# The low part's product ahead of the wide one in one block of every wide chunk

## The chip, the core and the metric

One Trainium2 chip, one NeuronCore of it. The kernel computes a whole two-part model block in one launch. The metric is the device time of a launch in microseconds; the median of the runs is quoted.

## The reference, cut to what matters

Two transformer-like blocks over 256 tokens of width 1024, all in fp32: a first one (gated feed forward of width 2816, latent and stick-breaking attention, a second gated feed forward, a gated projection) and a second one (short convolution, squared-ReLU feed forward of width 4096, sparse attention, another such feed forward, a final norm). What counts here are the dense products with weights:

```python
def swiglu(u, w_in, w_out):
    a, b = jnp.split(u @ w_in, 2, axis=-1)
    return (jax.nn.silu(a) * b) @ w_out

def squared_relu_mlp(h, w1, w2):
    return jnp.square(jax.nn.relu(h @ w1)) @ w2
```

They are wanted at nearly fp32 precision. The kernel reaches it by splitting: each fp32 operand is a high part (rounded to the fp32r format) and a low part (the rest), and a product is high x high + high x low + low x high.

## The kernel before, in words

**Weights.** All dense weights are packed into chunks of 128 partitions x 2048 fp32 (1 MB). Chunks are loaded in order into a ring of three slots `raw` by DMA from SyncE. ScalarE copies a chunk to its high part (`w_hi`, L438), VectorE subtracts to get the low part (`w_lo`, L858, semaphore `lo_split`), TensorE uses the chunk and counts `chunk_used` up, and ScalarE may overwrite the slot. Both parts lie in the tensor `w_hl`.

**Blocks.** A chunk that feeds the feed forwards holds 16 blocks of 128 x 128 weights. A block is either a `product` (L1625 to L1629): three matmuls of 256 columns, namely weights high with x high, weights high with x low, weights low with x high; or a `wide` (L1631 to L1635): one matmul of 512 columns, weights high with x high and x low side by side (L1634, 256 columns each, into a whole PSUM bank), and one of 256 columns, weights low with x high (L1635), added to the bank's first half. The two halves of the bank are added later by ScalarE and VectorE. Every matmul has its own weight load. `wide_low_first` (L1637 to L1641) is the same block with the two matmuls exchanged; both add to what an earlier block began, so it is never the first block of a bank.

**Wide chunks.** An up-chunk (`up`, L1706) makes two output tiles t = 0, 1 over eight input tiles k; the loops run over t and then k. In the first chunk of a stage the input x is only just being made, so `up` goes in four pieces, each behind a wait for the x piece (`op_lo`), with two k for each t in a piece. There are 22 up-chunks in ffn1 and ffn2 and 16 in mlp0 and mlp1. The second chunk of the program has a function of its own, `up_halves` (L1731), which uses `thirds` for four of its blocks. A down-chunk (`feed_forward`, L1791 to L1805) holds 16 consecutive blocks of a long list (output tile o outside, hidden tile f inside); there are 11 in ffn1, 11 in ffn2 and 16 in mlp0. mlp1's down projection (`last_down`) is built otherwise, from three 512-column matmuls (L1824 to L1826). Three output projections (`w_out`, `conv_out`, `nsa_out`) have four chunks each, three of them wide and one in the product form (`OUT_BANKS`, `NSA_OUT_BANKS`: a second entry of 0 marks the product form); they run through `out_tile`, `out_chunk`, `two_pairs` and, in the sparse attention, `out_piece` (L2221).

**Where the low part goes first now.** In the first chunk of `w_out` and `conv_out` (L1697), in the first up-chunk of ffn2, mlp0 and mlp1 (L1724), each at t = 0, k = 1, and in the first chunk of `nsa_out` at k = 4 (L2229). The instructions ahead of the three-matmul products and behind them are in the order of the code; TensorE executes its matmuls in that order. The waits stand at the head of a chunk (`arrived`, for `lo_split`, which is behind the whole low part) and of a piece, none between the two matmuls of a block.

## Time and profile before

| what | us |
|---|---|
| median of 3 runs (1194.53 to 1196.97) | 1195.65 |
| the profiled execution | 1195.6 |
| its span, first to last instruction | 1193.8 |
| TensorE busy in it | 1184.0 |
| VectorE, ScalarE, GpSimd busy | 859.2, 644.1, 226.9 |

The profile is of one execution. A matmul's start is recorded and its end modelled, so distances between starts are the firm numbers. The timeline gives starts to 0.01 us. PE is TensorE, PEld its weight loads, DVE VectorE, ACT ScalarE, POOL GpSimd.

### The profile page before, as it was taken

The page shows a single profiled execution, that of the slowest core. Times are in us where ns is not written, and L with a number is a line of the kernel's source. Part 1 is how long each engine was busy: PE and PEld are TensorE (multiplying, and loading weights), DVE is VectorE, ACT ScalarE, POOL GpSimd, SP SyncE. Part 2 cuts the span into 40 slices and gives each one's busy share as a digit, 9 for nine tenths or more (in the row PEclk, how much of TensorE's full clock was granted, in tenths as well). Part 3 has the DMA queues.
Part 4 walks back from the last instruction along what each step waited for, and adds up shares of the span by engine and source line. Part 5 has one row for each costly group of instructions (what it writes and reads, how often), then busy time and mean ns, then how long its engine had stood idle before and what let it go on. Part 6 is the DMA issues. An engine that isn't in the chain of part 4 may idle for free.

```text
span 1193.8 us, 19183 instructions
## 1 busy us (share of the span) xinstructions
PE 1184.0 (99%) x7641; PEld 1055.1 (88%) x7641; DVE 859.2 (72%) x1178; ACT 644.1 (54%) x860; POOL 226.9 (19%) x115
## 2 busy tenths in 40 slices
PE   9999999999999999999999999999999999999997
PEld 6888889988899888888999988888899978888886
DVE  6877767788868877766788786656578777766353
ACT  6655454465655755544643455444446784555432
POOL 1443301000000334310000024520000250455001
PEclk9999999999999999999999999999999999999999
DMA  8655555953245554555545555555576305555550
GB/s 319 212 180 198 186 177 187 275 209 107 106 151 180 178 208 177 194 194 182 177 161 186 187 204 206 179 197 192 181 278 233 121 19 177 186 202 178 184 202 36
DMA packets 31567, 218.03 MB, mean 183 GB/s; under 512 B 3584, under 2 KB 3856, under 8 KB 6272
## 3 DMA queue, kind: packets, MB, share of 16 engines
q1 hardware_dynamic: 29712, 210.07, 50.2%
q0 software_dynamic: 1488, 6.05, 1.8%
q8 instruction: 58, 0.95, 0.3%
q10 hardware_dynamic: 288, 0.79, 0.2%
q14 instruction: 21, 0.17, 0.0%
HBM read 215.82 MB, written 4.22 MB: 184 GB/s over the span
## 4 chain that ended last, share of the span: by engine, by line
PE 93%; DVE 4%; DMA 2%; ACT 1%; issue 1%; SPq 0%; DVEq 0%; ACTq 0%
PE bank L1634 38%; PE bank L1635 19%; PE bank L1627 7%; PE bank L1628 7%; PE bank L1629 7%; PE bank L1826 2%; PE bank L1825 2%; PE bank L1824 2%; DVE w_hl L858 1%; DMA raw<-weights 1%; PE bank L2081 1%; ACT w_hl L438 1%; PE bank L1975 0%; DMA par<-small 0%; PE bank L1755 0%
## 5 line engine op out<-in xcount | busy, mean ns | idle before, releaser
L858 DVE TENSOR_TENSOR w_hl<-raw,w_hl 128x2048 fp32r<-128x2048 f32 x194 | 444.0, 2289 | 134.1 <-ACT w_hl L438 133.2
L438 ACT ACTIVATE w_hl<-raw 128x2048 fp32r<-128x2048 f32 x195 | 370.5, 1902 | 135.8 <-PE bank L1635 46.6
L1634 PE MATMUL bank<-x_hl,w_hl 128*128 128x512 f32 x905 | 315.2, 394 | 0.2 <-DVE w_hl L1077 0.2
L377 POOL TENSOR_TENSOR hidden<-hid_f,hidden 128x256 fp32r<-128x256 f32 (+1 forms) x76 | 189.6, 2494 | 517.7 <-ACT hidden L521 306.0
L1635 PE MATMUL bank<-x_hl,w_hl 128*128 128x256 f32 x905 | 251.9, 278 | 0.0
L1634 PE MATMUL bank<-hidden,w_hl 128*128 128x512 f32 x608 | 210.9, 393 | 0.0
L1634 PEld LDWEIGHTS bank<-x_hl,w_hl 128*128 128x128 f32 x905 | 169.6, 187 | 39.1 <-DVE x_hl L908 0.7
L1635 PEld LDWEIGHTS bank<-x_hl,w_hl 128*128 128x128 f32 x905 | 170.4, 188 | 0.2
L1635 PE MATMUL bank<-hidden,w_hl 128*128 128x256 f32 x608 | 169.0, 278 | 0.0
L1634 PE MATMUL bank<-y_hl,w_hl 128*128 128x512 f32 x445 | 155.3, 395 | 0.0
L1627 PE MATMUL bank<-x_hl,w_hl 128*128 128x256 f32 x528 | 151.2, 286 | 0.1
L1629 PE MATMUL bank<-x_hl,w_hl 128*128 128x256 f32 x528 | 149.4, 283 | 0.0
L1628 PE MATMUL bank<-x_hl,w_hl 128*128 128x256 f32 x528 | 149.4, 283 | 0.0
L499 ACT ACTIVATE second<-bank 128x512 f32<-128x512 f32 (+1 forms) x100 | 54.4, 544 | 173.5 <-PE bank L1635 173.4
L1634 PEld LDWEIGHTS bank<-hidden,w_hl 128*128 128x128 f32 x608 | 113.9, 187 | 26.1
L1635 PE MATMUL bank<-y_hl,w_hl 128*128 128x256 f32 x445 | 123.6, 278 | 0.0
L1635 PEld LDWEIGHTS bank<-hidden,w_hl 128*128 128x128 f32 x608 | 114.4, 188 | 0.0
L1627 PEld LDWEIGHTS bank<-x_hl,w_hl 128*128 128x128 f32 x528 | 101.2, 192 | 2.0 <-issue 1.1
L1628 PEld LDWEIGHTS bank<-x_hl,w_hl 128*128 128x128 f32 x528 | 101.3, 192 | 0.1
L1629 PEld LDWEIGHTS bank<-x_hl,w_hl 128*128 128x128 f32 x528 | 101.3, 192 | 0.0
L1634 PEld LDWEIGHTS bank<-y_hl,w_hl 128*128 128x128 f32 x445 | 83.5, 188 | 19.2 <-issue 0.2
L958 DVE TENSOR_TENSOR t_ab<-bank,second 128x512 f32<-128x512 f32 x76 | 52.4, 690 | 64.2 <-ACT second L499 64.1
(397 smaller groups left out, 1713.6 us busy)
## 6 DMA issues: line engine op xcount, KB each, us to landing
raw<-weights SPq DMA_DIRECT2D x197, 1024.0 KB, 4.9
bias_skew<-bias_rows POOLq DMA_DIRECT2D x1, 3072.0 KB, 28.6
gate_or_bias<-bias_skew POOLq DMA_DIRECT2D x1, 2048.0 KB, 10.3
h<-x_t SPq DMA_DIRECT2D x2, 512.0 KB, 5.6
con<-consts SPq DMA_DIRECT2D x1, 769.5 KB, 12.7
raw<-weights ACTq DMA_DIRECT2D x1, 512.0 KB, 5.1
raw<-weights SPq DMA_DIRECT2D x1, 512.0 KB, 7.5
sv<-last_gain POOLq DMA_DIRECT2D x1, 512.0 KB, 4.0
```

Source lines behind the costliest of these rows:

```text
L377: nc.gpsimd.tensor_tensor(hidden[:, at, 1, :], src, hidden[:, at, 0, :].bitcast(F32), ALU.subtract).then_inc(hid_lo, 1)
L438: nc.scalar.activation(dst, src, ACT.Copy).then_inc(hi_split, 1)
L499: nc.scalar.activation(dst, src, ACT.Copy).then_inc(second_out, 1)
L858: V.tensor_tensor(w_lo[:, s, :], raw[:, s, :], w_hi[:, s, :].bitcast(F32), ALU.subtract).then_inc(lo_split, 1)
L958: V.tensor_tensor(t_ab[:, :, :], bank[:, s:s + 2, 0:S], second[:, j % 2, :, :], ALU.add).then_inc(ab_ready, 1)
L1627: mm(out_, w_hi[:, s, c:c + m], x[:, 0, :], start=start, stop=False, **kw)
L1628: mm(out_, w_hi[:, s, c:c + m], x[:, 1, :], start=False, stop=False, **kw)
L1629: return mm(out_, w_lo[:, s, c:c + m], x[:, 0, :], start=False, stop=stop, **kw)
L1634: mm(out_, w_hi[:, s, c:c + m], x, start=start, stop=False, **kw)
L1635: return mm(out_[:, 0:S], w_lo[:, s, c:c + m], x[:, 0, :], start=False, stop=stop, **kw)
L1824: mm(o, a, wh, start=f == 0, stop=False)
L1825: mm(o, a, wl, start=False, stop=False)
```

## The change

`wide` gets a flag `low_first`. With it the block issues the 256-column product with the low part first and the 512-column one behind it. The separate function goes, and the special places in `two_pairs`, `up` and `out_piece` with it. The flag is set in one block of every wide chunk: at t = 0, k = 1 in the up-chunks and output projections, at the second block of each down-chunk. `up_halves` does not set it.

```diff
--- before.py
+++ after.py
@@ -1628,17 +1628,14 @@
                 mm(out_, w_hi[:, s, c:c + m], x[:, 1, :], start=False, stop=False, **kw)
                 return mm(out_, w_lo[:, s, c:c + m], x[:, 0, :], start=False, stop=stop, **kw)
 
-            def wide(out_, s, c, m, x, start, stop):
+            def wide(out_, s, c, m, x, start, stop, low_first=False):
 
                 kw = dict(skip_group_check=True)
+                if low_first:
+                    mm(out_[:, 0:S], w_lo[:, s, c:c + m], x[:, 0, :], start=False, stop=False, **kw)
+                    return mm(out_, w_hi[:, s, c:c + m], x, start=False, stop=stop, **kw)
                 mm(out_, w_hi[:, s, c:c + m], x, start=start, stop=False, **kw)
                 return mm(out_[:, 0:S], w_lo[:, s, c:c + m], x[:, 0, :], start=False, stop=stop, **kw)
-
-            def wide_low_first(out_, s, c, m, x):
-
-                kw = dict(skip_group_check=True)
-                mm(out_[:, 0:S], w_lo[:, s, c:c + m], x[:, 0, :], start=False, stop=False, **kw)
-                return mm(out_, w_hi[:, s, c:c + m], x, start=False, stop=False, **kw)
 
             def thirds(out_, s, c, m, x, start, stop):
 
@@ -1673,7 +1670,8 @@
                 if banks[1] == 0:
                     return product(bank[:, banks[0], t * S:(t + 1) * S], s, k * 256 + t * P, P, x[:, k, :, :],
                                    start and t == 0, stop, skip_group_check=True)
-                return wide(bank[:, banks[0] + t * banks[1], :], s, k * 256 + t * P, P, x[:, k, :, :], start, stop)
+                return wide(bank[:, banks[0] + t * banks[1], :], s, k * 256 + t * P, P, x[:, k, :, :], start, stop,
+                            t == 0 and k == 1)
 
             def out_chunk(banks, s, x):
 
@@ -1694,9 +1692,6 @@
                                 pe.wait_ge(op_lo, PC[pieces] + p + 1)
                             for t in range(2):
                                 for k in range(KT // n * p, KT // n * (p + 1)):
-                                    if j == 0 and t == 0 and k == 1 and banks[j][1] > 0:
-                                        last = wide_low_first(bank[:, banks[j][0], :], c % RING, 256, P, x[:, 1, :, :])
-                                        continue
                                     last = out_tile(banks[j], (c + j) % RING, t, k, x, k == 0, k == KT - 1)
                         if b == n:
                             last.then_inc(chunk_used, 1)
@@ -1709,7 +1704,7 @@
                     for t in range(2):
                         for k in range(KT):
                             last = wide(bank[:, 2 * slot + t, :], s, k * 256 + t * P, P, x[:, k, :, :], k == 0,
-                                        k == KT - 1)
+                                        k == KT - 1, t == 0 and k == 1)
                     return last
                 n = NP[pieces]
                 for p in range(n):
@@ -1721,11 +1716,8 @@
                             arrived(1)
                     for t in range(2):
                         for k in range(KT // n * p, KT // n * (p + 1)):
-                            if t == 0 and k == 1 and not first:
-                                last = wide_low_first(bank[:, 2 * slot, :], s, 256, P, x[:, 1, :, :])
-                                continue
                             last = wide(bank[:, 2 * slot + t, :], s, k * 256 + t * P, P, x[:, k, :, :], k == 0,
-                                        k == KT - 1)
+                                        k == KT - 1, t == 0 and k == 1)
                 return last
 
             def up_halves(slot, x):
@@ -1798,7 +1790,8 @@
                         pe.wait_ge(hid_lo, b + f * UPS[stage] // nf + 1)
                     if f == 0 and o >= 5:
                         pe.wait_ge(h_upd, upd + o - 3)
-                    ins = wide(bank[:, DOWN_BANKS[o], :], c % RING, i % 16 * P, P, hidden[:, f, :, :], f == 0, ended)
+                    ins = wide(bank[:, DOWN_BANKS[o], :], c % RING, i % 16 * P, P, hidden[:, f, :, :], f == 0, ended,
+                                   i % 16 == 1)
                     if i % 16 == 15:
                         ins.then_inc(chunk_used, 1)
                     elif ended:
@@ -2226,9 +2219,6 @@
                 pe.wait_ge(op_lo, PC["o_nsa"] + p + 1)
                 for t in range(2):
                     for k in range(KT // n * p, KT // n * (p + 1)):
-                        if j == 0 and t == 0 and k == 4:
-                            last = wide_low_first(bank[:, NSA_OUT_BANKS[j][0], :], c % RING, 4 * 256, P, y_hl[:, 4, :, :])
-                            continue
                         last = out_tile(NSA_OUT_BANKS[j], c % RING, t, k, y_hl, k == 0, k == KT - 1)
                 if p == n - 1:
                     last.then_inc(chunk_used, 1)
```

## Rows read from the trace of the kernel before

**Rows 1.** The page's head: span, busy times, the 40 slices, granted clock (tenths)

```profile
span 1193.8 us, 19183 instructions
...
PE 1184.0 (99%) x7641; PEld 1055.1 (88%) x7641; DVE 859.2 (72%) x1178; ACT 644.1 (54%) x860; POOL 226.9 (19%) x115
...
PE   9999999999999999999999999999999999999997
...
PEclk9999999999999999999999999999999999999999
```

**Rows 2.** The page's chain of waits, by engine and line, and TensorE's list of waits

```profile
PE 93%; DVE 4%; DMA 2%; ACT 1%; issue 1%; SPq 0%; DVEq 0%; ACTq 0%
PE bank L1634 38%; PE bank L1635 19%; PE bank L1627 7%; PE bank L1628 7%; PE bank L1629 7%; PE bank L1826 2%; PE bank L1825 2%; PE bank L1824 2%; DVE w_hl L858 1%; DMA raw<-weights 1%; PE bank L2081 1%; ACT w_hl L438 1%; PE bank L1975 0%; DMA par<-small 0%; PE bank L1755 0%
...
PE bank L1853 <- POOL relb L365: 2.3, 1, 2.3
```

**Rows 3.** The page's groups of instructions: the wide block's matmul by moving operand

```profile
L1634 PE MATMUL bank<-x_hl,w_hl 128*128 128x512 f32 x905 | 315.2, 394 | 0.2 <-DVE w_hl L1077 0.2
...
L1634 PE MATMUL bank<-hidden,w_hl 128*128 128x512 f32 x608 | 210.9, 393 | 0.0
...
L1634 PE MATMUL bank<-y_hl,w_hl 128*128 128x512 f32 x445 | 155.3, 395 | 0.0
```

**Rows 4.** One source line (L1640, low part ahead): its matmuls, ns min/median/max, first and last start

```profile
L1640 PE MATMUL bank<-x_hl,w_hl x3: 282/285/286, 365.2 to 1009.1; 128*128 128x256 f32 x3
...
L1640 PE MATMUL bank<-y_hl,w_hl x3: 285/285/386, 387.6 to 988.8; 128*128 128x256 f32 x3
```

**Rows 5.** TensorE's timeline (start us, duration us), ffn1's up-chunks, steady

```profile
60.34 0.39 PE L1634 MATMUL bank<-x_hl,w_hl 128*128 128x512 f32 x1
60.57 0.28 PE L1635 MATMUL bank<-x_hl,w_hl 128*128 128x256 f32 x1
...
132.45 0.39 PE L1634 MATMUL bank<-hidden,w_hl 128*128 128x512 f32 x1
```

**Rows 6.** TensorE's timeline, first chunk of the output projection `w_out`, with the form

```profile
364.87 0.40 PE L1634 MATMUL bank<-x_hl,w_hl 128*128 128x512 f32 x1
...
365.22 0.29 PE L1640 MATMUL bank<-x_hl,w_hl 128*128 128x256 f32 x1
365.34 0.40 PE L1641 MATMUL bank<-x_hl,w_hl 128*128 128x512 f32 x1
365.58 0.40 PE L1634 MATMUL bank<-x_hl,w_hl 128*128 128x512 f32 x1
...
370.44 0.39 PE L1634 MATMUL bank<-x_hl,w_hl 128*128 128x512 f32 x1
```

**Rows 7.** TensorE's timeline, last chunk of `w_out` (products) and first of ffn2

```profile
381.54 0.28 PE L1627 MATMUL bank<-x_hl,w_hl 128*128 128x256 f32 x1
...
383.32 0.28 PE L1627 MATMUL bank<-x_hl,w_hl 128*128 128x256 f32 x1
...
387.28 0.40 PE L1634 MATMUL bank<-y_hl,w_hl 128*128 128x512 f32 x1
...
392.86 0.38 PE L1763 MATMUL bank<-sq,ones 128*128 128x256 f32 x1
```

**Rows 8.** TensorE's timeline, chunk 0 of ffn1, second and third block

```profile
10.05 0.40 PE L1634 MATMUL bank<-x_hl,w_hl 128*128 128x512 f32 x1
...
10.40 0.39 PE L1634 MATMUL bank<-x_hl,w_hl 128*128 128x512 f32 x1
```

**Rows 9.** TensorE's timeline, last down projection, 512-column matmuls in a row

```profile
1100.76 0.39 PE L1824 MATMUL bank<-w_hl,hidden 128*128 128x512 f32 x1
...
1101.44 0.39 PE L1824 MATMUL bank<-w_hl,hidden 128*128 128x512 f32 x1
```

**Rows 10.** TensorE's timeline, mlp1's first chunk, and the instruction after it

```profile
1008.74 0.40 PE L1634 MATMUL bank<-x_hl,w_hl 128*128 128x512 f32 x1
...
1014.38 0.38 PE L1763 MATMUL bank<-sq,ones 128*128 128x256 f32 x1
```

## Prediction

> **What bounds the kernel now.** I read the head of the page first: TensorE is busy 1184.0 of 1193.8 us, its busy row has 9 in every slice but the last, and the granted clock is at the 2.4 GHz level all along [rows 1]. The chain of waits says the same of the end: 93% of it is TensorE, and 57% is the two lines of the wide block alone; the list of waits has a single long one for TensorE, 2.3 us at the start [rows 2]. So TensorE never stands idle for data, nearly every nanosecond put on or taken off its stream moves the end, and no other engine can take the bound for a change of less than a per cent. The costs of this change must be read from the distances between starts of matmuls, not from busy times, because the ends are modelled and a busy TensorE can still be in a slower rhythm.
>
> The groups of instructions give the number of wide blocks in the usual order: 905 + 608 + 445 = 1958 [rows 3]; the low-first form stands six times (three and three) [rows 4].
>
> The steady rhythm: the low matmul starts 0.23 us after the wide one, and 13 chunks of 16 blocks lie between 60.34 and 132.45 us: 72.11 / 13 = 5.547 us a chunk, 0.3467 us a block [rows 5]. At 2.4 GHz 512 + 256 columns are 0.320 us; 0.0267 is left, 0.0133 for each matmul. ScalarE and VectorE split a chunk and update tiles beside all of this, and the rhythm does not move, so I take it for TensorE's own.
>
> **The change, part by part.** (a) No instruction is added or removed. Weights, moving operands, banks, waits and increments are the same; in one block of a chunk two neighbours change places. The wait for the chunk's low split stands ahead of the whole chunk, so the low part is there when it is read first: no new wait, and no transfer or queue is moved. Cost 0; what hides it is that wait itself, and if it came late (by row it never does) both orders would wait alike.
>
> (b) The count. Afterwards the form stands in 21 of ffn1's 22 up-chunks (the second goes through `up_halves`, not touched), in 22, 16 and 16 of the other stages, in 11 + 11 + 16 down-chunks and in 3 wide chunks of each of three output projections: 75 + 38 + 9 = 122, against six now. 116 are new. One of the six moves, in the attention's output projection, from the fifth input tile to the second; it stays one block, and I give the move nothing (bounds: the price of one block either way, 0.03 us).
>
> (c) The price of one. The order high, low, high, low becomes high, low, low, high, high, low: a short-to-long and a long-to-short transition give way to a short-to-short and a long-to-long one. Both new transitions exist elsewhere, in steady streams. Short-to-short, in the three-matmul product: 33 matmuls from 383.32 to 387.28 us, 0.120 each [rows 7]. Long-to-long, in the last down projection: 0.68 for three, 0.227 each [rows 9]. The sum is 0.347, which is what the pair takes now. That is the lower end: **0 a block**. I exclude a gain as a term of the sum since all three streams have the same 0.0133 over the pure columns; a gain is a rival below.
>
> The upper end is a chunk that has the form now. From 364.87 to 370.44 us is 5.57 [rows 6], from 387.28 to 392.86 is 5.58 [rows 7]; two more, at 669.88 and 692.30, repeat it. The mean, 5.575, is **0.028 over** the steady chunk. In the rows the surplus sits right behind the swap: the low matmul put first takes 0.12, the long one behind it 0.24 until the next long one, where 0.227 is the steady distance [rows 6]. But these four all follow a stream of three-matmul products, and such a border has a cost of its own. In the other direction it gives time back: from 381.54 (the last wide chunk has ended) to 387.28 us are 48 matmuls in 5.74 us, where 48 x 0.120 is 5.76, so 0.02 is gained [rows 7]. If entering costs what leaving gives, 0.008 is left for the swap. A start without the form, chunk 0 behind its wait, shows a second block of 0.35 against 0.347, next to nothing for entering [rows 8]; then the swap bears it all. So 0.008 to 0.028 by this, 0 by the transitions. I take **0.012**, near the border read backwards, since that is the same border, and a little above it for the 0.24 us directly at the swap.
>
> Sum: 116 x 0.012 = 1.4 us. All of it lies on the path, as TensorE is the path. The slow rhythm described next is not counted as cured. The profiled execution took 1195.6 us (1193.8 span and 1.8 around it), and the median of the three is 1195.65, so the sum stands against either: **1197.0 us**.
>
> A rule to weigh: in the steady product stream, where every matmul has its own weight load, the distance is 0.120 us, so a load costs no more than that beside a 256-column matmul [rows 7]. The Trainium skill, "TensorE: Matmul & The Clock Gate", section "LDWEIGHTS (loading the stationary operand)", gives columns / 1.2 ns for a load, for 128 columns some 107 ns (an estimate), which would just fit under a 256-column matmul in either order; by it the swap is free and the time 1195.6 us. The chunks with the form do not bear that out in full.
>
> **The rivals.** About 0.2% (2.4 us) is what a measurement of this kernel can tell from no change.
> - *Order is free* (the steady streams). 0 x 116: 1195.6. For it: three streams with one overhead. Against it: the four chunks at 5.575. Chance 0.20.
> - *The swap bears the whole surplus* (ends on the slower side). Place: the two or three long matmuls after each swap. 116 x 0.028 = 3.2 us, 1198.8. It passes 0.2% from 0.021 a block on. For it: chunk 0 enters without a surplus. Against: leaving gains 0.02. Chance 0.18.
> - *The swap tips TensorE into the slow rhythm.* The chunk from 1008.74 to 1014.38 took 5.64, 0.093 over the steady one, though it holds the form [rows 10]; about four chunks in a row there run so, and the stream ahead of it was slow already. If swaps set it off for good it is 122 x 0.093 = 11.3 us, 1207; if in a third of the chunks, 3.8 us, 1199.4. For it: two of the six blocks of now stand in slow stretches. Against: both stretches were slow before the block, and four blocks are followed by the steady rhythm. Chance 0.12.
> - *A better rhythm.* Curing the slow chunks seen gives 4 x 0.093 = 0.4 us, not measurable. Over 0.2% faster takes 1.2 ns off each of 1964 blocks, below the 0.0133 that no steady stream here undercuts, or other executions with much more of the slow rhythm. About 1192.5. Chance 0.10.
> - *The change does not do what it says*: a block that is skipped. The count (b) would show it; it costs nothing, and is part of the free case.
>
> **How the numbers follow.** The forecast, small cost, has 0.40; most of it ends within 0.2% (up to 0.021 a block, 1198.0). Same: nearly all of 0.40 and 0.20, less the tails, 0.55. Slower: 0.18, 0.12 and a tail of the forecast, 0.33. Faster: 0.12. The range takes in the free case and the full surplus, with the run-to-run spread of 1 us below, and the slow rhythm in up to a third of the chunks above: 1194.2 to 1199.8.
>
> **What would show it.** Counts of the form: 122 and a line of 512 columns with 1842 blocks beside it. TensorE's share unchanged, and its waits too. Each chunk of the up and down stages from its first start to the next's: 5.547 (free), 5.559 (forecast), 5.575 (full surplus), 5.64 (slow rhythm). The prediction is wrong if that chunk is outside 5.547 to 5.575, and wrong in its idea if time comes or goes in stages without wide blocks, or if TensorE begins to wait.

## The result, and the profile after

The changed kernel is slower. Its median is 1207.8 us (six runs, 1205.56 to 1208.74) against 1196.07 for the kernel before (six runs, 1194.53 to 1196.98): a ratio of 1.0089, interval 1.0075 to 1.0104. The forecast of 1197.0 and its range (up to 1199.8) are missed; the time is the one that the rival of the slow rhythm gave, 1207.

The page of the changed kernel: its head, and the shares of the engines in the chain of waits.

```profile
span 1206.4 us, 19183 instructions
...
PE 1197.3 (99%) x7641; PEld 1061.5 (88%) x7641; DVE 859.2 (71%) x1178; ACT 644.3 (53%) x860; POOL 226.9 (19%) x115
...
PEclk9999999999999999999999999999999899999999
...
PE 99%; DVE 0%; ACT 0%; POOL 0%; issue 0%; DVEq 0%; POOLq 0%
```

Against [rows 1] the span is 12.6 us longer, TensorE is busy 13.3 us longer with the same 7641 matmuls, and VectorE and GpSimd are busy exactly as long as before. TensorE's list of waits still has one line, as in [rows 2]:

```profile
PE bank L1846 <- POOL relb L365: 2.4, 1, 2.4
```

So no new wait took the time. Next, the wide block's long matmul among the page's groups, and the line of the swapped low product (ns min/median/max, first and last start). They answer to [rows 3, 4].

```profile
L1637 PE MATMUL bank<-x_hl,w_hl 128*128 128x512 f32 x852 | 303.7, 398 | 0.0
...
L1637 PE MATMUL bank<-hidden,w_hl 128*128 128x512 f32 x570 | 203.0, 399 | 0.0
...
L1637 PE MATMUL bank<-y_hl,w_hl 128*128 128x512 f32 x420 | 150.0, 399 | 0.0
```

```profile
L1635 PE MATMUL bank<-x_hl,w_hl x56: 278/282/285, 10.2 to 1105.3; 128*128 128x256 f32 x56
...
L1635 PE MATMUL bank<-hidden,w_hl x38: 282/282/283, 134.8 to 874.8; 128*128 128x256 f32 x38
...
L1635 PE MATMUL bank<-y_hl,w_hl x28: 278/283/285, 390.8 to 1008.7; 128*128 128x256 f32 x28
```

The count is as predicted: 56 + 38 + 28 = 122 swapped blocks, 852 + 570 + 420 = 1842 in the usual order. What is new is the mean of the *unswapped* ones, 398 and 399 ns where it was 393 to 395. The change did not touch these blocks, and yet most of the time was lost on them. TensorE's timeline shows it (start us, duration us), a chunk well inside ffn1's up-chunks, and two later chunk starts:

```profile
66.61 0.40 PE L1637 MATMUL bank<-x_hl,w_hl 128*128 128x512 f32 x1
66.85 0.28 PE L1638 MATMUL bank<-x_hl,w_hl 128*128 128x256 f32 x1
66.97 0.28 PE L1635 MATMUL bank<-x_hl,w_hl 128*128 128x256 f32 x1
67.09 0.40 PE L1636 MATMUL bank<-x_hl,w_hl 128*128 128x512 f32 x1
67.32 0.40 PE L1637 MATMUL bank<-x_hl,w_hl 128*128 128x512 f32 x1
...
72.26 0.40 PE L1637 MATMUL bank<-x_hl,w_hl 128*128 128x512 f32 x1
...
128.79 0.40 PE L1637 MATMUL bank<-x_hl,w_hl 128*128 128x512 f32 x1
```

From 66.61 to 128.79 us are 11 chunks: 62.18 / 11 = 5.653 us, where [rows 5] give 5.547. The recorded starts are finer than the timeline's two digits, and taken in ns they show repeating patterns. From each start to the next, h for a 512-column matmul and l for a 256-column one:

| name in the text below | pattern, ns | a block | a chunk of 16 |
|---|---|---|---|
| one-block rhythm | h230 l117 | 346.7 | 5.547 |
| two-block rhythm | h231 l113, h233 l117 | 346.7 | 5.547 |
| slow rhythm, of three blocks | h241 l120, h236 l113, h233 l117 | 353.3 | 5.653 (or 5.661, 5.649, 5.650 in turn) |

The kernel before runs nearly all its wide chunks in one of the first two. In the changed one, 101 chunks of the four feed forwards are in the third: all from the fifth chunk on in ffn1, and from the fourth on in ffn2, mlp0 and mlp1. The trace shows the way in, at the second chunk of a stretch (27.05 us; the distances in ns are h230 l117, swap l118 h233, then h230 l114 h232 l118 **h241 l120**):

```profile
27.05 0.39 PE L1637 MATMUL bank<-x_hl,w_hl 128*128 128x512 f32 x1
...
27.40 0.28 PE L1635 MATMUL bank<-x_hl,w_hl 128*128 128x256 f32 x1
27.52 0.40 PE L1636 MATMUL bank<-x_hl,w_hl 128*128 128x512 f32 x1
27.75 0.39 PE L1637 MATMUL bank<-x_hl,w_hl 128*128 128x512 f32 x1
```

At the swap itself next to nothing is lost: from 27.05 to 27.75 us two blocks take 0.70, near their 0.693. The slow rhythm begins two blocks on and then holds; the next chunk's swap does not break it.

**Where the 12.6 us are.** ffn1 and ffn2, before and after, as TensorE's busy time and clock in their windows (the columns: window, its length, busy time and count of PE, PEld, DVE, ACT, POOL, clock granted, DMA share, GB/s). Before:

```profile
9.60:193.50 183.90, 183.87 (x1063) 162.02 (x1064) 139.75 (x172) 105.26 (x134) 49.00 (x22) 1.00 0.59 210
387.30:570.80 183.50, 183.50 (x1061) 160.43 (x1060) 136.79 (x169) 102.57 (x128) 49.92 (x22) 1.00 0.54 190
```

After:

```profile
9.70:196.60 186.90, 186.90 (x1064) 162.49 (x1063) 139.93 (x172) 105.13 (x133) 49.00 (x22) 1.00 0.58 206
390.40:577.20 186.80, 186.80 (x1060) 162.18 (x1059) 137.17 (x169) 102.56 (x128) 49.93 (x22) 1.00 0.53 186
```

The clock is granted in full in all four, and the same work takes 3.1 us more in ffn1 (183.83 and 186.94 from first start to last) and 3.3 in ffn2 (183.50 and 186.80); mlp0 takes 3.2 more (177.95 and 181.14). mlp1's up-chunks add 1.5 (89.27 to 90.75), the two output projections 0.4, and the stretches without wide blocks nothing, but for one: that is 11.45 us in all. It fits the pattern: 101 chunks x 0.106 = 10.7 us. The first chunks of the stages and the output projections add 0.9 to it, and 0.2 goes off, because the profiled execution of the kernel before stalled at one chunk border of ffn1 (37.8 to 38.4 us: l218 h336) and the other one did not. The last 1.2 us are in the stretch that holds the sparse attention (107.02 to 108.20, up to the start of its output projection), and there it is the clock. The same view, of that stretch before and after:

```profile
939.00:943.00 4.00, 4.00 (x25) 3.09 (x26) 2.59 (x7) 0.71 (x2) 2.50 (x2) 0.71 0.92 356
```

```profile
949.00:952.00 3.00, 3.00 (x15) 2.67 (x17) 1.35 (x4) 0.30 (x1) 2.02 (x2) 0.50 0.98 355
952.00:956.00 4.00, 4.00 (x22) 3.26 (x19) 3.37 (x20) 1.76 (x7) 0.00 (x0) 0.55 0.15 57
```

The clock falls to its 1.2 GHz level for 3.4 us in the execution before (from 940.7 us) and for 6.8 us in the one after (from 948.8). The experiments show that this varies from execution to execution, whatever the order of the blocks.

### The profile page after: what moved, and what is told of

Read it like the earlier page. It is cut to its first block, busy times and chain, and to the rows that moved or that the text cites. A ratio compares the mean times of both kernels' runs of the same rounds, so it can differ in the third digit from the quotient of the medians.

```text
span 1206.4 us, 19183 instructions
## 1 busy us (share of the span) xinstructions
PE 1197.3 (99%) x7641; PEld 1061.5 (88%) x7641; DVE 859.2 (71%) x1178; ACT 644.3 (53%) x860; POOL 226.9 (19%) x115
## 4 chain that ended last, share of the span: by engine, by line
PE 99%; DVE 0%; ACT 0%; POOL 0%; issue 0%; DVEq 0%; POOLq 0%
PE bank L1637 36%; PE bank L1638 18%; PE bank L1627 8%; PE bank L1628 8%; PE bank L1629 8%; PE bank L1817 2%; PE bank L1818 2%; PE bank L1819 2%; PE bank L1636 2%; PE bank L1635 1%; PE bank L2074 1%; PE bank L1747 1%; PE bank L1749 1%; PE bank L1748 1%; PE bank L1846 1%; PE bank L1968 0%
## 5 line engine op out<-in xcount | busy, mean ns | idle before, releaser
L1637 PE MATMUL bank<-x_hl,w_hl 128*128 128x512 f32 x852 | 303.7, 398 | 0.0
L1638 PE MATMUL bank<-x_hl,w_hl 128*128 128x256 f32 x852 | 239.2, 281 | 0.0
L1637 PE MATMUL bank<-hidden,w_hl 128*128 128x512 f32 x570 | 203.0, 399 | 0.0
L1637 PEld LDWEIGHTS bank<-x_hl,w_hl 128*128 128x128 f32 x852 | 160.0, 188 | 36.3
L1638 PEld LDWEIGHTS bank<-x_hl,w_hl 128*128 128x128 f32 x852 | 160.9, 189 | 2.8
L1638 PE MATMUL bank<-hidden,w_hl 128*128 128x256 f32 x570 | 160.1, 281 | 0.0
L1627 PE MATMUL bank<-x_hl,w_hl 128*128 128x256 f32 x528 | 151.1, 286 | 0.1
L1637 PE MATMUL bank<-y_hl,w_hl 128*128 128x512 f32 x420 | 150.0, 399 | 0.0
L1628 PE MATMUL bank<-x_hl,w_hl 128*128 128x256 f32 x528 | 149.4, 283 | 0.0
L1629 PE MATMUL bank<-x_hl,w_hl 128*128 128x256 f32 x528 | 149.4, 283 | 0.0
L1637 PEld LDWEIGHTS bank<-hidden,w_hl 128*128 128x128 f32 x570 | 107.1, 188 | 24.7
L1638 PE MATMUL bank<-y_hl,w_hl 128*128 128x256 f32 x420 | 117.9, 281 | 0.0
L1638 PEld LDWEIGHTS bank<-hidden,w_hl 128*128 128x128 f32 x570 | 107.6, 189 | 1.9
L1627 PEld LDWEIGHTS bank<-x_hl,w_hl 128*128 128x128 f32 x528 | 101.1, 191 | 2.0 <-issue 1.1
L1628 PEld LDWEIGHTS bank<-x_hl,w_hl 128*128 128x128 f32 x528 | 101.2, 192 | 0.1
L1629 PEld LDWEIGHTS bank<-x_hl,w_hl 128*128 128x128 f32 x528 | 101.1, 192 | 0.0
L1637 PEld LDWEIGHTS bank<-y_hl,w_hl 128*128 128x128 f32 x420 | 78.9, 188 | 18.1 <-issue 0.3
```

What stands on the lines that cost most here:

```text
L1627: mm(out_, w_hi[:, s, c:c + m], x[:, 0, :], start=start, stop=False, **kw)
L1628: mm(out_, w_hi[:, s, c:c + m], x[:, 1, :], start=False, stop=False, **kw)
L1629: return mm(out_, w_lo[:, s, c:c + m], x[:, 0, :], start=False, stop=stop, **kw)
L1637: mm(out_, w_hi[:, s, c:c + m], x, start=start, stop=False, **kw)
L1638: return mm(out_[:, 0:S], w_lo[:, s, c:c + m], x[:, 0, :], start=False, stop=stop, **kw)
```

## The experiments

**The theory** after the result: a swap in a steady stream sets off the slow rhythm, and it holds until something ends it; the cost lies in the chunks behind. **The local rival**: each swap costs its own 0.09 us, in its chunk. **The outside rival**: the stages are slower through something else in the changed kernel, and swaps have no part in it. Lengths of chunks and stages are from the traces. The total of the kernel before spreads from 1193.5 to 1200.0 us over these sets, so that a total alone cannot show two microseconds well; where the two differ, I go by the trace.

**One swap more, in ffn1.** The kernel before with one more swapped block, k = 1 of up-chunk 10.

```diff
+SWAPPED = {("ffn1", 10): ((0, 1),)}
...
+                            if (t, k) in swapped:
+                                last = wide_low_first(bank[:, 2 * slot + t, :], s, k * 256 + t * P, P, x[:, k, :, :], k == KT - 1)
+                                continue
```

> The kernel before with one more block swapped: ffn1's up-chunk 10, second block. Rhythm theory (TensorE's stream has several steady rhythms; a swap moves it from one to another, and the slow one, 5.653 us a chunk against 5.547, then keeps itself going in the usual order until something breaks it): from chunk 10 on, the 12 up-chunks and 11 down-chunks of ffn1 run at 5.65 us each though no block in them but one is swapped: 23 x 0.107 = +2.4 us, and ffn2, mlp0 and mlp1 are as before. Local theory (a swap costs about 0.1 us where it stands, in its own chunk): chunk 10 takes 5.65, the next ones 5.547, and the whole is +0.1 us, not measurable.

Median 1197.77, ratio 0.9999 (0.9982 to 1.0017): the total shows nothing. The trace does. Starts of chunks 10, 11 and 14, on TensorE's timeline:

```profile
66.31 0.39 PE L1635 MATMUL bank<-x_hl,w_hl 128*128 128x512 f32 x1
...
71.95 0.40 PE L1635 MATMUL bank<-x_hl,w_hl 128*128 128x512 f32 x1
...
88.91 0.40 PE L1635 MATMUL bank<-x_hl,w_hl 128*128 128x512 f32 x1
```

Chunk 9 took 5.547. Chunk 10 took 5.631 us, and all 22 chunks of ffn1 behind it, which hold no swap, take 5.661, 5.649 or 5.650; ffn1 is 186.34 us long where 183.9 is usual for the same chunk 0. ffn2 and mlp0 keep their 5.547. In this execution one swap costs 2.4 us, nearly all of it in chunks without any: the theory's case, and both rivals fall. But it does not do so in every execution: four of the ten times are 1193.7 to 1194.8, among the lowest of the kernel before (1193.57), and have no room for 2.4 us; the interval of the ratio ends below the 1.002 that 2.4 us would be. The profiles to come show how that can be.

**The same swap in ffn2**, and **in two chunks running**.

```diff
+SWAPPED = {("ffn2", 10): ((0, 1),)}
```

> The kernel before with one more block swapped: ffn2's up-chunk 10, second block. In the trace before, ffn2 runs in a third rhythm: same 5.547 us a chunk, but its distances repeat every two blocks (231, 113, 233, 117 ns), where ffn1's repeat every block (230, 117). Rhythm theory with a map read from the changed kernel (a swap leads from the two-block rhythm to the one-block rhythm, and from that to the slow one): chunk 10 costs 0.012 us more, and from there distances are 230, 117; no chunk is at 5.65; total 0.0 us. Rhythm theory without the map (any swap in a fast rhythm leads to the slow one): 23 chunks slow, +2.4 us. Local theory: +0.1 us in chunk 10 alone.

```diff
+SWAPPED = {("ffn2", 10): ((0, 1),), ("ffn2", 11): ((0, 1),)}
```

> The kernel before with two more blocks swapped: ffn2's up-chunks 10 and 11, second block of each. Rhythm theory with the map: chunk 10 as in the run with one swap (0.01 us), the second swap leads to the slow rhythm, so chunks 11 to 21 and the 11 down-chunks take 5.65: about 22 x 0.107 = +2.3 us. Local theory: +0.2 us, in the two chunks alone. Without the map: about +2.4 us, slow from chunk 10.

One swap: 1197.03, ratio 1.0003 (0.9985 to 1.002). Two: 1197.93, ratio 1.0022 (1.0008 to 1.0036). Chunk starts with one swap in ffn2:

```profile
443.78 0.39 PE L1635 MATMUL bank<-y_hl,w_hl 128*128 128x512 f32 x1
...
449.34 0.39 PE L1635 MATMUL bank<-y_hl,w_hl 128*128 128x512 f32 x1
...
454.89 0.39 PE L1635 MATMUL bank<-y_hl,w_hl 128*128 128x512 f32 x1
```

and with two:

```profile
443.22 0.39 PE L1635 MATMUL bank<-y_hl,w_hl 128*128 128x512 f32 x1
...
448.77 0.39 PE L1635 MATMUL bank<-y_hl,w_hl 128*128 128x512 f32 x1
...
454.41 0.40 PE L1635 MATMUL bank<-y_hl,w_hl 128*128 128x512 f32 x1
```

A single swap here costs 0.012 us (5.559, then 5.547 for good): the theory as I had put it was too simple. The ns tell why. ffn2 was in the two-block rhythm, and the first swap led to the one-block rhythm, equally fast. The second swap found the one-block rhythm, as in ffn1, and led to the slow one: 5.632, then 5.661, 5.649, 5.650 to the end, ffn2 185.84 us for 183.50. Here the total agrees: none of the ten times is under 1197.15, and the interval takes in the 1.002. What a swap does hangs on the rhythm that it meets.

**All swaps out**, the six that the kernel before has.

```diff
-                                    if j == 0 and t == 0 and k == 1 and banks[j][1] > 0:
-                                        last = wide_low_first(bank[:, banks[j][0], :], c % RING, 256, P, x[:, 1, :, :])
-                                        continue
...
```

> The kernel before with none of its six swaps: all wide blocks in the usual order. Rhythm theory: the border from the three-matmul product into wide blocks now leads somewhere else; if the six swaps were of use, the wide chunks behind each border (three of w_out, ffn2's first, three of conv_out, mlp0's first, those of nsa_out, mlp1's first) run at 5.65 until the sum of squares breaks the rhythm: +0.5 to +1 us. Local theory: six swaps fewer, -0.17 us at most (0.028 each) by my prediction's upper price, -0.6 us by 0.1 each.

Median 1197.98, ratio 1.0014 (0.9998 to 1.003). Behind each stretch of three-matmul products the wide chunks are now slow: `w_out` 5.651, 5.661, 5.649 (with its swap 5.572, 5.547, 5.546), ffn2's first chunk 5.653 for 5.573, and the same in `conv_out` and mlp0. `w_out` takes 16.96 us for 16.67. The stretch ends where ffn2's sum of squares breaks in. So four of the six swaps of the kernel before cure a slow rhythm, and the surplus of 0.028 that I read off them is the time until the cure takes, not a price of the swap. The other two, in `nsa_out` and in mlp1's first chunk, cure it in some executions only: these two places take 14.22 and 5.638 us in the profile before, 13.98 and 5.574 in that of the single swap in ffn1, and 14.24 and 5.654 with all swaps out.

**A break behind the swap.** The first experiment's kernel, with an fp32 matmul of ones and squares of 256 columns ahead of ffn1's chunk 14, like the one in each stage's sum of squares.

```diff
+                    if stage == "ffn1" and j == 14:
+                        mm(bank[:, 6, 0:S], ones[:, :], sq[:, 0, :], start=True, stop=True)
```

> The kernel before with ffn1's up-chunk 10 swapped in its second block (as in the first run, which went slow from there to the end of ffn1), and one small fp32 matmul of 256 columns (ones times a tile of squares, into a bank nobody reads) in front of up-chunk 14. Nothing else. Rhythm theory: the extra matmul does what the sum of squares does after chunk 1, and ends the slow rhythm: chunks 10 to 13 at 5.63 to 5.66 us, then one with a stall of some 0.4 us around the extra matmul, and all from 14 on at 5.547; ffn1 gets back 19 x 0.105 = 2.0 us of the 2.4, less the stall. A rival in which the swap changes something in the memory or in the chunk's position that stays (the ring, the banks): slow to the end of ffn1 in spite of the matmul.

1195.27 us in a single run. Chunks 10 to 13 take 5.631, 5.661, 5.649 and 5.653. The break, on the timeline:

```profile
88.81 0.28 PE L1636 MATMUL bank<-x_hl,w_hl 128*128 128x256 f32 x1
88.93 0.38 PE L1786 MATMUL bank<-sq,ones 128*128 128x256 f32 x1
```

Chunk 14 begins at 89.17 and takes 5.739, with 0.42 us at its first matmul where 0.23 is usual; every chunk behind it takes 5.547. ffn1 is 184.74 us long: 0.41 for four slow chunks, 0.24 for the added matmul and 0.19 for the pause, against the 2.44 of the first experiment. The slow rhythm is a state that a break can end, not a price of later blocks.

**Swaps in chunks 10 and 13 of ffn1**, three chunks apart, to meet the slow rhythm at another place.

```diff
+SWAPPED = {("ffn1", 10): ((0, 1),), ("ffn1", 13): ((0, 1),)}
```

> The kernel before with two blocks swapped in ffn1: second block of up-chunk 10 and second block of up-chunk 13. In the slow rhythm distances repeat every three blocks (241+120, 236+113, 233+117 ns); a chunk has 16 blocks, so in chunk 13 the second block comes behind the (233, 117) one, a place in the cycle at which no swap has been seen yet. The changed kernel's swaps all came behind the (241, 120) one and stayed slow. If the rhythm's state is its place in the cycle, this swap can lead elsewhere: 5.547 from chunk 13 or 14 on (I give that 1 in 2), otherwise 5.65 to the end of ffn1. Local theory: both chunks 5.65, all others 5.547, which the first run has excluded.

1197.89 us, a single run. The premise failed: in this execution ffn1 ran in the two-block rhythm. The swap in chunk 10 led to the one-block rhythm (5.561, then 5.547), the one in chunk 13 to the slow one (5.631, then slow to the end). It repeats the pair in ffn2 and says nothing on a swap inside the slow rhythm; that went to the next three. It would also account for the four low times of the first experiment (no trace of those runs was kept): where an execution runs ffn1 in the two-block rhythm, the swap in chunk 10 costs 0.014 us. Which of the two it is in ffn1 is a matter of the execution; at this place the profiles have both.

**Two swaps a chunk, and eight.** The changed kernel with the flag also at k = 4, and, in another, at every second block.

```diff
-                                        k == KT - 1, t == 0 and k == 1)
+                                        k == KT - 1, t == 0 and k in (1, 4))
...
-                                   i % 16 == 1)
+                                   i % 16 in (1, 4) and f > 0)
```

> The changed kernel with twice as many swaps: in every wide chunk the second and the fifth block (of the first output tile). Behind a swap that comes in the one-block rhythm, the fifth block is the one behind (233, 117), the place not yet tried. If a swap there leads out of the slow rhythm, most chunks take 5.55 to 5.60 us and the total is 2 to 3 us over the kernel before, under the changed kernel's, although there are twice the swaps. If it does not, chunks stay at 5.65 and the total is the changed kernel's, +11 to +12 us. A price per swap, of whatever size, says +23 us.

```diff
-                                        k == KT - 1, t == 0 and k == 1)
+                                        k == KT - 1, k % 2 == 1)
...
-                                   i % 16 == 1)
+                                   i % 2 == 1)
```

> The changed kernel with every second block swapped (all odd input tiles, and every odd block of a down-chunk), eight per chunk: long, short, short, long, long, short, short, long. A price per swap of 0.1 us says +0.8 us a chunk, +95 us in all. Rhythm theory: no price per swap; this order has a steady rhythm of its own, which no run has shown: between 5.547 us a chunk (the sum of the steady short-to-short and long-to-long distances, 0.120 + 0.227) and the slow 5.653, so 0 to +12 us.

Two a chunk: 1200.0, ratio 1.0021 (1.0008 to 1.0034). Eight: 1198.6, ratio 1.0016 (1.0006 to 1.0025). More swaps than the change has, and three quarters of its loss or more are gone. In both, the steady chunk takes 5.573, 0.027 over the fast one. In the first, the swap at k = 1 starts the slow rhythm, and the one at k = 4, three blocks on and just behind the pair h233 l117, ends it: l121 h238 h235 l116 h235 l117 h230, the same distances as where a swap cures the stream behind a product border. One chunk in ffn1 and one in ffn2 have no second swap (the flag is left out at a bank's first block, `f > 0`), and just these take 5.631 and 5.632, and the next ones 5.595. The other kernel settles in a rhythm of its own that never reaches the 241.

**TensorE by itself.** The kernel before, and behind its last matmul some 210 us in which, but for the first five, only TensorE works, on data already in place: series of 22 to 25 blocks with a swap between, after a pause; then the low product in another bank, another moving tile for it, the same shapes in bf16, and series behind 16 three-matmul products. The added part computes nothing that is put out.

```diff
+            for n in (22, 23, 24):
+                reset()
+                usual(24, plain, True)
+                swap(plain)
+                usual(24, plain)
+                swap(plain)
+                usual(n, plain)
+                swap(plain)
+                usual(24, plain)
...
```

> The kernel before, and behind its last matmul a series of blocks for TensorE alone (their results go into banks nobody reads; 22 stretches, some 180 us longer), when the other engines have only the last updates to do and are then idle. Each series begins with one small fp32 matmul, which ends any rhythm; then 24 blocks in the usual order, a swapped one, 24, a second swapped one. (1) Three series of the kernel's own form, with a third swap behind 22, 23 or 24 further blocks, so that it falls at each of the three places of the slow cycle. Rhythm theory: distances of a block 346.7 ns, after the first swap 346.7, after the second 353.3, with nobody else at work; and one of the three third swaps (the one behind the 233, 117 block) leads back to 346.7, the other two stay at 353.3. If the slow rhythm came from ScalarE's or VectorE's traffic, all stretches are at 346.7. (2) The low product into another bank; the low product with another tile as its moving operand; the same shapes in bf16. If the rhythm is one of the weight loads against the streaming columns, the first two change nothing, and the bf16 one, which the warm-up matmuls show with 215 ns for 512 columns and so no 0.0133 us overhead, has no slow rhythm. (3) 16 three-matmul products, then wide blocks with and without a swap: without 353.3, with 346.7 (as in the run without any swap).

The same two speeds appear to the ns with all other engines idle, 346.7 and 353.3 a block. Over the three series and two variants, a swap met the two-block rhythm and led to the one-block rhythm; met the one-block rhythm and led to the slow one; met the slow rhythm behind h233 l117 and led to the one-block rhythm; and behind h236 l113 or h241 l120 left it slow. The swaps did not come in the order that I had expected, because the matmul ahead of each series left the stream slow once, in the two-block rhythm twice and in the one-block rhythm twice. A slow-to-fast case (the swap is L2292 and L2293) and the fast-to-slow one behind it:

```profile
1198.32 0.28 PE L2296 MATMUL bank<-hidden,w_hl 128*128 128x256 f32 x1
1198.44 0.28 PE L2292 MATMUL bank<-hidden,w_hl 128*128 128x256 f32 x1
1198.56 0.40 PE L2293 MATMUL bank<-hidden,w_hl 128*128 128x512 f32 x1
...
1207.13 0.28 PE L2292 MATMUL bank<-hidden,w_hl 128*128 128x256 f32 x1
1207.25 0.40 PE L2293 MATMUL bank<-hidden,w_hl 128*128 128x512 f32 x1
...
1213.47 0.40 PE L2295 MATMUL bank<-hidden,w_hl 128*128 128x512 f32 x1
1213.71 0.28 PE L2296 MATMUL bank<-hidden,w_hl 128*128 128x256 f32 x1
```

Another bank and another moving tile change nothing in this. bf16 has no such states: 216 and 109 ns, 325 a block, with swaps and without. Behind the products one plain block and a swap give the fast rhythm, no swap the slow one. The profile's loads differ too, in the answer on the line of the long product:

```profile
L2295 PEld LDWEIGHTS bank<-hidden,w_hl x479: 187/188/192, 1189.8 to 1400.8; 128*128 128x128 f32 x160
...
L2295 PEld LDWEIGHTS bank<-zeros x72: 96/98/98, 1346.8 to 1370.6; 128*128 128x128 bf16 x72
```

**The other 1.2 us: the half clock.** The fall at 940.7 us stands behind a row of 32 matmuls of 14 columns in the sparse attention, which begins at 936.6. Here they are spread among 24 matmuls of the value product that ran just ahead of them; the work is the same.

```diff
-            value(0).then_inc(chunk_used, 1)
+            value(0, (0,))
...
+                    if q == 0:
+                        mm(o2, a, wh, start=t == 0, stop=False, **kw)
+                        mm(o2, a, wl, start=False, stop=False, **kw)
...
+                last = mm(o2, b, wh, start=False, stop=t == KT - 1, **kw)
+            last.then_inc(chunk_used, 1)
```

> The kernel before; of the sparse attention, the 32 matmuls of 14 columns (3.6 us, in which TensorE moves hardly any columns) are no longer in one row but spread among the 24 matmuls of 256 columns that stood ahead of them. Nothing is added or left out. In the runs so far TensorE's clock stood at half (1.2 GHz) for 0, 3.4 or 6.8 us right behind that row of small matmuls, and the stretch between the wide chunks around it took 105.9, 107 or 108 to 109 us. If the row of small matmuls is what lets the clock fall: no fall, 105.7 to 106 us in every run, and the whole 1193.5 to 1194.5 with a small spread, 0.2% under the median of the kernel before. If the fall has another cause (the wait a few us ahead of it): the same spread as before, 1193.6 to 1200.

> The kernel of the run before this once more, for a firmer ratio: nine of its twelve times lay at 1193.5 to 1194.4 and three at 1196.6 to 1197.1, where the kernel before spreads over 1193.5 to 1199.9. If the spread small matmuls keep the clock up for good: the profile shows no half clock around 940 us, no time over 1198, a median of 1194 to 1195, ratio 0.998. If the first set was luck: times of 1198 and more appear, and a half clock in that stretch.

The same kernel in two sets: 1194.17, ratio 0.999 (0.9976 to 1.0003), and 1195.11, ratio 0.9993 (0.9982 to 1.0004); neither interval leaves out 1, and the small spread that I had expected did not come. The window that held the fall, in the first of them, has the clock in full with TensorE less busy:

```profile
938.00:942.00 4.00, 3.74 (x31) 3.12 (x30) 2.58 (x5) 1.72 (x3) 3.48 (x2) 1.00 0.94 369
```

The stretch takes 105.74 and 105.88 us for 107.02. In the unmixed kernels above it took 105.8 us where the clock did not fall (all swaps out), 106.7 with 3.4 us of half clock (two swaps in ffn2) and 109.1 with 6.8 (one swap in ffn1): the fall is a matter of the execution. Seven of the ten unmixed profiles (all but the probe's) have it, and none of the five mixed ones. The runs without a profile say the same by their mean granted clock: 0.998 or 0.999 in all 52 executions of the mixed kernels, 0.996 or 0.997 in 39 of the 68 of the kernel before that ran beside four of these sets. The times of this kernel fall in two groups, 16 of 24 at 1193.5 to 1195.2 and 8 at 1196.6 to 1197.3, and the second set's profile is of the upper one. It shows why, at a chunk border of ffn1 with no swap in it anywhere:

```profile
38.01 0.28 PE L1635 MATMUL bank<-x_hl,w_hl 128*128 128x256 f32 x1
38.14 0.39 PE L1634 MATMUL bank<-x_hl,w_hl 128*128 128x512 f32 x1
...
43.78 0.40 PE L1634 MATMUL bank<-x_hl,w_hl 128*128 128x512 f32 x1
```

From 38.01 the border took 122 ns, where the first set's profile has 119 at this place and goes on fast, and the 28 chunks behind it are slow: ffn1 186.60 us instead of 183.9. By these two traces a few nanoseconds at the wrong place do what a swap does; no run set that delay on purpose.

**The changed kernel with the mixed attention.**

> The changed kernel with its 32 small matmuls of the sparse attention spread in the same way. The changed kernel's profile had 6.8 us of half clock there, the one of before 3.4 us: 1.2 of its 12.6 us of span. Rhythm theory: with the clock out of the way what is left of the change is the slow rhythm, 11.3 to 11.5 us: span of the profile 1203.5 to 1204, time 1205.3 to 1205.8, each chunk 5.653. If the difference of the two profiles had another part: more or less than that.

1206.92 (four runs, 1205.84 to 1207.22), ratio 1.009 (1.0072 to 1.0109). No half clock in that stretch, and the four wide stages take 186.93, 186.80, 181.14 and 90.75 us, as in the changed kernel. With the clock taken out of it the loss stands. The sum that I had expected was 1 us short: the span is 1204.9 us, 12.4 over the first mixed set's 1192.5. Of these, 11.7 are in the stages and output projections with wide blocks, and some 0.6 lie ahead of ffn1 and in the first attention, where the two executions differ.

**Two ways to guard ffn1**, on the mixed kernel: the fp32 matmul ahead of chunk 7, and pairs of swaps in chunks 7, 8 and 9.

```diff
+                    if stage == "ffn1" and j == 7:
+                        mm(bank[:, 6, 0:S], ones[:, :], sq[:, 0, :], start=True, stop=True)
```

> The kernel with the small matmuls spread, and one small fp32 matmul of 256 columns in front of ffn1's up-chunk 7 (ones times a tile of squares, into a bank nobody reads), as in the run with the breaker. The last profile showed the slow rhythm without any added swap: a few ns of delay at the end of ffn1's chunk 4 set it off, and the 29 chunks from 5 on took 5.65, +2.9 us; that would be the upper group of its times (5 of 12 at 1196.8 to 1197.3 against 1194.1 to 1195.2). If so: the matmul costs 0.2 us and brings ffn1 back to 5.547 in every execution, the upper group goes, all times lie within 1.2 us, median 1194.0 to 1195.0, ratio to the kernel before 0.998. If the upper group has another cause (the start of the weights' stream, say), 3 to 5 of 12 times stay 2.9 us above the others.

```diff
+SWAPPED = {("ffn1", j): ((0, 1), (0, 4)) for j in (7, 8, 9)}
```

> The kernel with the small matmuls spread, without the extra fp32 matmul, and with the second and fifth block swapped in ffn1's up-chunks 7, 8 and 9. From the map of the runs so far: two swaps three blocks apart lead from the fast rhythm back to the fast one (0.027 us a chunk), and from the slow one to the fast one (where the second comes behind the 233, 117 block), whatever the ns; the fp32 matmul did not, it led into the slow one in the last profile. So ffn1 from chunk 10 on at 5.547 in all executions, whether or not a delay in chunk 4 set off the slow rhythm: the upper group of times (7 of 12 last time) goes, all times within 1.2 us, median 1194.0 to 1195.0, ratio 0.998. If pairs do not lead out of the slow rhythm from every place in its cycle, an upper group of some executions stays, 2.5 us above.

The break missed: 1197.34, ratio 0.9999 (0.9988 to 1.0011), with 7 of 12 runs at 1197.3 or more. In its profile the added matmul itself leads to the slow rhythm. Its line and the matmuls behind it:

```profile
49.55 0.59 PE L1782 MATMUL bank<-sq,ones 128*128 128x256 f32 x2
49.79 0.58 PE L1634 MATMUL bank<-x_hl,w_hl 128*128 128x512 f32 x1
50.21 0.28 PE L1635 MATMUL bank<-x_hl,w_hl 128*128 128x256 f32 x1
50.33 0.40 PE L1634 MATMUL bank<-x_hl,w_hl 128*128 128x512 f32 x1
50.57 0.28 PE L1635 MATMUL bank<-x_hl,w_hl 128*128 128x256 f32 x1
```

From 50.33 to 50.57 is the 0.241 of the slow rhythm; ffn1 takes 186.94. Such a break throws the state anew, it does not set it: in the earlier experiment it came out fast, here slow, and in the probe all three rhythms came out of it.

The pairs hold: 1194.29 us (12 runs, 1193.55 to 1195.78), ratio 0.9986 (0.9975 to 0.9997), and none of the 12 at 1196.6 or more, where the same kernel without them has 8 of 24. The spread is 2.2 us, though, and not the expected 1.2. Its profile has 5.627, 5.595 and 5.573 us for the three chunks, 0.15 us in all, and 5.547 behind them. It also corrects what I expected of a pair: ffn1 ran in the two-block rhythm, and there the first pair ended in the slow rhythm (one swap to the one-block rhythm, the next to the slow one); the second pair ended it. It is the one kernel here whose ratio to the kernel before has an interval wholly below 1, by 0.14% in the middle. That gain is of pairs and mixed attention together; a direct comparison with the mixed kernel alone was not made.

## Why the prediction was wrong

What bounds the kernel held: TensorE is the path, no wait came in, and the costs have to be read from the distances of starts. One reading was wrong and changed nothing in the sum: the granted clock was not at its upper level all along, it was halved for 3.4 us from 940.7 us on, which the tenths of a 30 us slice do not show. Parts (a) and (b) held to the instruction.

**The step that failed is (c), the price of one.** It took 5.575 us of a chunk with the form [rows 6, 7] as the steady 5.547 [rows 5] and a surplus of the swap and the border, and split it. Both halves of that were wrong, and so was the term in the sum, 116 x 0.012 us. With the swaps out, the same chunks take 5.65: the 0.028 was what remained of a slow rhythm until the swap had cured it. And all four rows were of one case, a swap just behind products. Nearly all of the 116 new swaps stand in steady streams, of which the trace of before holds no example at all. The bounds of 0 to 0.028 were worked out from rows on every side, but of another case, and what the changed kernel showed lay outside them: 0.106 us in each of 101 chunks, in a slow rhythm that the swaps set off. It is also no price of a swap: measured alone, one costs 0.012 or 2.4 us, by the rhythm that it meets, and two in a chunk cost 0.027 together. That the 0.012 is the very figure of the forecast is luck: it was taken from a product border, and it holds for a swap in the two-block rhythm alone.

**The lower end**, the sum of steady transitions, named a mechanism that TensorE does not follow here. The usual order, the same transitions in the same number, takes 5.547 or 5.653 us a chunk. The Trainium skill's figure for a weight load that went with it ("TensorE: Matmul & The Clock Gate", section "LDWEIGHTS (loading the stationary operand)"), some 107 ns by the estimate, made the order free; the result is 11.7 us over the kernel before. In the probe the recorded load of a bf16 tile is 98 ns, near it, and that of an fp32r tile 188.

**The rival of the slow rhythm** came true, with its sum: 122 x 0.093 = 11.3 us forecast, 11.45 found between the traces, though as 101 chunks at 0.106 and a rest. I gave it 0.12. The argument against it was that both slow stretches had been slow before their block and that four blocks are followed by the steady rhythm. The second half is true, and by the runs it says something else: those four swaps cure a slow rhythm. The first half was read from lengths of chunks and does not hold in ns. In `nsa_out` the swap (988.76 us) is the first wide block behind a row of 128-column matmuls; in mlp1's first chunk [rows 10] it stands one block behind 48 products, which in this execution ran 121, 120, 124, 118, 117 ns where other executions have 120 nearly throughout. Directly ahead of neither stands a slow stretch of wide blocks, and behind both the 241 and 120 of the slow pattern set in within six blocks. These distances were there to be read in the trace of before. They do not convict the swap either: with all swaps out the two places are slow too.

**The range** reached up to the slow rhythm in a third of the chunks. A state that holds by itself is in all of them or in few; a third was no case of its own. What the prediction said would prove it wrong did so: a chunk outside 5.547 to 5.575.

**What stays open.** Why TensorE has these rhythms. Other engines, the bank and the moving tile are ruled out by the probe, and the rhythms are absent in bf16. That the longer weight load of fp32r (188 ns beside matmuls 117 and 230 apart) makes the order matter would fit, but it is argued and not shown: no run changed the load alone. Nor was it settled which length of a pause leads where, or why ffn1 comes in the one rhythm or the other.

## What to carry to other kernels

A price read off a place is the price at that place. Ask what the stream was doing in the rows that carry an estimate, and how many of them are of the situation that the edit will make; where it is none, a rival that needs no new mechanism, only a state already seen in the trace, deserves far more than a tenth. When a bound engine streams without waits, compare its distances in ns and look for patterns before means, and measure one instance of the edit in one stage by the trace: a swap of two matmuls here showed 2.4 us in one stage's length, where the total showed nothing. Then ask whether the times of the other executions have room for what the one trace shows: here four of ten had not, since what the edit costs depends on a state that the execution brings along.

## What the runs showed of the hardware

- Alternating 512- and 256-column fp32r matmuls, each with its own weight load, run on TensorE in stable rhythms of 346.7 or 353.3 ns a pair at the same full clock. The slow state lasts up to the end of a stage (28 chunks without any swap, some 160 us). A swap or a pause changes the state, and by two traces a border 3 ns late did.
- An fp32r matmul costs on average 13.3 ns above its columns at 2.4 GHz in the fast rhythms (346.7 = 320 + 2 x 13.3), a bf16 one 2.5 (216 + 109 = 325). The Trainium skill, "TensorE: Matmul & The Clock Gate", section "Wait — 56ns, not 53.3ns?", has 2.5 ns for a matmul; the bf16 series agrees and the fp32r streams do not.
- The clock fell to 1.2 GHz for 3.4 or 6.8 us, in some executions, behind a row of 32 matmuls of 14 columns, though TensorE counts as busy throughout. With these spread among matmuls of 256 columns none of 52 executions had the fall (105.7 to 106.0 us for the stretch, where those with a fall have 106.7 to 109.1).
